# Two of the twelve adaptive-modulation parts moved from TensorE to VectorE, and their loads into the feed-forward stage

## The reference

```python
mod = jax.nn.silu(c) @ w_ada[l] + b_ada[l]                     # 1024 -> 6 * 1024
sh_m, sc_m, gt_m, sh_f, sc_f, gt_f = jnp.split(mod, N_MOD, axis=-1)
h = modulate(rms_norm(x, g_mix[l]), sh_m, sc_m)
y = token_mixer(h, ...)        # dilated attention and an mLSTM, joined, times w_out
x = x + gt_m[:, None, :] * y
h = modulate(rms_norm(x, g_ffn[l]), sh_f, sc_f)
x = x + gt_f[:, None, :] * swiglu(h, w_gate[l], w_up[l], w_down[l])   # inner width 2816
```

## Time and profile before

| | us |
|---|---|
| median of 3 runs (1412.06 to 1413.28) | 1412.82 |
| the profiled execution | 1411.05 |
| its span, first to last instruction | 1409.0 |
| TensorE busy in it | 1273.0 (90%) |
| VectorE busy | 726.7 (52%) |
| ScalarE busy | 238.8 (17%) |
| GpSimd busy | 324.6 (23%) |

### The profile page before, as it was taken

The page is one execution under the profiler, slowest core; times in us unless marked ns, Lnnn a source line. Parts: engine busy times, 40 slices in busy tenths (PEclk is TensorE's granted clock), DMA queues, the critical chain, the costliest instruction groups (busy, mean ns, idle before and its releaser), DMA issues.

```text
span 1409.0 us, 12608 instructions
## 1 busy us (share of the span) xinstructions
PE 1273.0 (90%) x4558; PEld 730.9 (52%) x4558; DVE 726.7 (52%) x1752; ACT 238.8 (17%) x611; POOL 324.6 (23%) x273
## 2 busy tenths in 40 slices
PE   7999999988988878788799887878999899999998
PEld 6757554574554444333333333333465468988743
DVE  3664623178777777787786865653255242100001
ACT  2132221121111111112221112112112421000000
POOL 0100000024544544354444454540000000000000
PEclk9999999999999999899999998999999989999999
DMA  8534576369999999999999999995344723552530
GB/s 289 176 123 180 179 277 245 120 269 421 390 419 421 421 416 420 416 421 401 417 422 421 411 415 421 420 422 216 120 166 166 263 78 120 179 180 95 204 145 34
DMA packets 98380, 398.72 MB, mean 283 GB/s; under 512 B 6353, under 2 KB 9809, under 8 KB 65425
## 3 DMA queue, kind: packets, MB, share of 16 engines
q0 software_dynamic: 37376, 270.29, 46.4%
q1 hardware_dynamic: 60944, 127.65, 25.4%
HBM read 396.86 MB, written 1.05 MB: 282 GB/s over the span
## 4 chain that ended last, share of the span: by engine, by line
PE 60%; DMA 22%; DVE 12%; issue 2%; ACT 2%; POOL 1%; DVEq 0%; SPq 0%; ACTq 0%
DMA big<-in_peer_uv,idx_t 21%; PE ps L497 16%; PE ps L509 14%; PE ps L747 11%; DVE big L1763 6%; PE ps L998 5%; PE ps L716 2%; PE ps L686 2%; PE ps L962 2%; PE ps L523 1%; PE ps L589 1%; POOL big L1364 1%; PE ps L486 1%; DMA wring<-in_w_ada 1%; ACT rows L1185 1%
## 5 line engine op out<-in xcount | busy, mean ns | idle before, releaser
L747 PE MATMUL ps<-big,rows 128*128 128x512 f32 x1024 | 489.0, 634 | 105.4 <-ACT rows L1185 105.4
L1364 POOL DMA_INDIRECT big<-in_peer_uv,idx_t x256 | 312.0, 1219 | 388.9 <-PE ps L747 323.5
L747 PEld LDWEIGHTS ps<-big,rows 128*128 128x128 f32 x1024 | 202.7, 203 | 374.0 <-issue 374.0
L1763 DVE CUSTOM_DVE_ANT_0 big<-big 128x1024 f32<-128x1024 f32 x256 | 307.8, 1225 | 145.5 <-DMA big<-in_peer_uv,idx_t 142.5
L497 PE MATMUL ps<-wring,big 128*128 128x512 f32 (+1 forms) x560 | 240.5, 586 | 2.6 <-DMA wring<-in_w_in 1.1
L509 PE MATMUL ps<-big,wring 128*128 128x256 f32 x896 | 195.7, 381 | 1.0 <-DVE big L1418 1.0
L509 PEld LDWEIGHTS ps<-big,wring 128*128 128x128 f32 x896 | 171.2, 191 | 25.3 <-issue 1.9
L497 PEld LDWEIGHTS ps<-wring,big 128*128 128x128 f32 x560 | 105.6, 191 | 125.8 <-issue 121.0
L1179 ACT ACTIVATE small<-small 128x4 f32<-128x4 f32 x64 | 13.2, 206 | 514.7 <-DVE small L1768 514.7
L1185 ACT ACTIVATE rows<-const,small 128x128 f32<-128x128 f32 x256 | 81.8, 390 | 19.2 <-DVE small L1772 18.0
L998 PE MATMUL ps<-wring,big 128*128 128x512 f32 x176 | 75.7, 592 | 0.0
(11 more groups left out here) (241 smaller groups left out, 921.9 us busy)
## 6 DMA issues: line engine op xcount, KB each, us to landing
wring<-in_w_in SPq DMA_DIRECT2D x17, 2048.0 KB, 8.3
wring<-in_w_ada SPq DMA_DIRECT2D x12, 2048.0 KB, 8.5
wring<-in_w_gate SPq DMA_DIRECT2D x5, 2048.0 KB, 7.7
wring<-in_w_up SPq DMA_DIRECT2D x5, 2048.0 KB, 7.7
wring<-in_w_down SPq DMA_DIRECT2D x5, 2048.0 KB, 7.6
wring<-in_w_out SPq DMA_DIRECT2D x4, 2048.0 KB, 15.1
wring<-in_peer_wq SPq DMA_DIRECT2D x4, 2048.0 KB, 8.0
big<-in_peer_uv,idx_t POOLq DMA_INDIRECT x256
```

What stands on the lines that cost most here:

```text
L747: last = nc.tensor.matmul(banks[h], diag[:, k % DIAGS, :], v_part[:, ring_at(k), h * 512:(h + 1) * 512], start=False, stop=(k % SLOTS == S ...
L1364: pool.indirect_dma_start(pair_ring[:, ring_at(k), :], None, a["peer_uv"], bass.IndirectOffsetOnAxis(idx_t[:, k:k + 1], 0))\
L1763: nc.vector.tensor_tensor_reduce(u_part[:, ring_at(k), :], u_part[:, ring_at(k), :], h_t[:, b, :], 1.0, 0.0, ALU.mult, ALU.add, a_dot[:, i ...
```

## The change

- The tiles ada10 and ada11 leave their place behind ada9 in the list of loads. ada10 now stands behind up1 and ada11 behind up2 (`FF_ADA = {1: 10, 2: 11}`), in the same ring.
- TensorE no longer computes them. DVE does, by `gate_part`: behind its work on gate1/up1 (and on gate2/up2) it waits for the tile and runs one tensor_scalar and seven scalar_tensor_tensor over 128 x 512 elements, each multiplying a 128-row slice of the tile with its column of silu(c) and adding to mod_part(i). Each of the eight waits for the one before.
- The sum over the 128 rows is still a matmul, with ones in all rows as the stationary operand (`one.to_broadcast([P, P])`), behind up2 for part 10 and behind up3 for part 11. ACT moves its result behind its tanh of gate2 and gate3.
- SP's wait for the slot of an ada tile is on the new semaphore ada_made, which DVE raises.
- POOL raises mod_ready after each of its two additions; DVE needs the first before gt_m is used and the second before the last additions.
- As the list of products is shorter by ada10 and ada11 in the mixer and has ada_row 10 and 11 later, all products behind m_S get other banks.

```diff
+FF_ADA = {1: 10, 2: 11}
...
-    t += [("in2_og", KD, 512, "w_in_2", 0, 512 * 6)] + ada[8:12]
+    t += [("in2_og", KD, 512, "w_in_2", 0, 512 * 6)] + ada[8:10]
...
         t += [(f"gate{i}", KD, w, "w_gate", 0, 512 * i), (f"up{i}", KD, w, "w_up", 0, 512 * i)]
+        if i in FF_ADA:
+            t += [ada[FF_ADA[i]]]
...
                     before = TILES[n - W_SLOTS][0]
-                    if before.startswith("down"):
+                    if before in ("ada10", "ada11"):
+                        sp.wait_ge(ada_made, int(before[3:]) - 9)
+                    elif before.startswith("down"):
...
             def ada_row(i):
 
-                wait_moved(pe, f"ada{i}")
+                if i >= 10:
+                    pe.wait_ge(ada_made, i - 9)
+                else:
+                    wait_moved(pe, f"ada{i}")
                 o = begin("ada_row", i)
-                nc.tensor.matmul(o, group_sum, mod_part(i), start=True, stop=True).then_inc(product_done, 1)
+                nc.tensor.matmul(o, one.to_broadcast([P, P]) if i >= 10 else group_sum, mod_part(i), start=True,
+                                 stop=True).then_inc(product_done, 1)
...
-            ada_part(10)
-            ada_part(11)
             ada_row(8)
             ada_row(9)
...
             attended(0)
-            ada_row(10)
-            ada_row(11)
             probs_turned(1)
...
                 by_cols(f"up{i}", TILES[TILE_NO[f"up{i}"]][2], hT2)
+                if i - 1 in FF_ADA:
+                    ada_row(FF_ADA[i - 1])
...
-            ada_moves(10)
-            ada_moves(11)
             move(mod_part(8), "ada_row", 8)
...
-                if b:
-                    move(mod_part(10), "ada_row", 10)
-                    move(mod_part(11), "ada_row", 11)
...
                     nc.scalar.activation(ff_e, bank((f"gate{i}", h)), ACT.Tanh, scale=0.5).then_inc(ff_exp, 1)
+                if i - 1 in FF_ADA:
+                    move(mod_part(FF_ADA[i - 1]), "ada_row", FF_ADA[i - 1])
...
-                if j == 0:
-                    link(last)
-            last.then_inc(mod_ready, 1)
+                last.then_inc(mod_ready, 1)
+                pool.wait_ge(mod_ready, j + 1)
...
+            def gate_part(i):
+
+                n = TILE_NO[f"ada{i}"]
+                slot = n % W_SLOTS * TILE
+                w = wring[:, slot:slot + TILE].rearrange("p (c n) -> p c n", c=KD)
+                to = mod_part(i)
+                dve.wait_ge(tile_landed[n % W_SLOTS], 16 * (n // W_SLOTS + 1))
+                link(ts(to, w[:, 0, :], c_s[:, 0:1], None, ALU.mult))
+                for c in range(1, KD - 1):
+                    link(stt(to, w[:, c, :], c_s[:, c:c + 1], to, ALU.mult, ALU.add))
+                stt(to, w[:, KD - 1, :], c_s[:, KD - 1:KD], to, ALU.mult, ALU.add).then_inc(ada_made, 1)
...
+                if i in FF_ADA:
+                    gate_part(FF_ADA[i])
+            dve.wait_ge(mod_ready, 2)
```

More of the change, by code:

```diff
@@ L175, in product_list @@
     p += [("m_cols",), ("m_M", 0), ("m_M", 1)] + [("m_S", h) for h in range(GH)]
-    p += [("ada10",), ("ada11",), ("ada_row", 8), ("ada_row", 9)]
-    p += [("d_PT", 0, 0, q) for q in range(2)] + [("d_Y", 0), ("ada_row", 10), ("ada_row", 11)]
+    p += [("ada_row", 8), ("ada_row", 9)]
+    p += [("d_PT", 0, 0, q) for q in range(2)] + [("d_Y", 0)]
     p += [("d_PT", 1, sb, q) for sb in range(NB) for q in range(2)]
@@ L186, in product_list @@
             p += cols(n, 2 if i < 5 else 1)
+        if i - 1 in FF_ADA:
+            p += [("ada_row", FF_ADA[i - 1])]
     p += [("down", b, h) for b in range(NB) for h in range(2)]
@@ L379, in two_blocks @@
         ple_exp, mod_ready, x_ready = sem("ple_exp"), sem("mod_ready"), sem("x_ready")
-        modc_ready = sem("modc_ready")
+        modc_ready, ada_made = sem("modc_ready"), sem("ada_made")
         d_norm, d_max, d_probs, cat_ready = sem("d_norm"), sem("d_max"), sem("d_probs"), sem("cat_ready")
```

## The result

| | before | after |
|---|---|---|
| median, us | 1413.10 (6 runs, 1412.06 to 1413.68) | 1403.65 (6 runs, 1401.05 to 1406.13) |
| the profiled execution, us | 1411.05 | 1404.53 |
| its span, us | 1409.0 | 1402.7 |
| ratio, 95% interval | | 0.9932 (0.9919 to 0.9945) |

The changed kernel is 9.5 us faster by the medians, 6.5 by the two profiled executions. The forecast was 1405.5 in 1402.2 to 1409.0.

The account below looks back on a forecast made before the run. TensorE, busy 1273 of 1409 us, was taken as the bound, with a chain of waits at the mixer's end. 1411.05 - 9.1 (mixer chain) + 1.8 (clock) + 1.8 (row sums) = 1405.5 us, range 1402.2 to 1409.0.

Parts of the forecast that it names:

- ada10 and ada11 out of the mixer: Mixer's end on TensorE: without these parts and their row sums there, m_num 0 starts 8.35 us earlier.
- the 0.2 counted against the gain: Mixer, d_Y 0: ACT's four moves take 2.1 us, so it starts at about 1116.4 and not 1116.2.
- POOL's hold: DVE's small tensor_scalar before the second division waits for POOL's bias addition; moving that gains 0.75 us, m_den 1 late next.
- Row sums: Feed-forward stage on TensorE, which has no gap: two row sums return at 0.9 us each, +1.8 us, perhaps not hidden.
- DVE's parts: Feed-forward stage on DVE: eight steps of 0.69 us, 5.8 us a part, covered by 112 us of idle time, cost 0.
- The loads: Feed-forward stage: tiles ada10 and ada11 delay no gate load, at least 6 us of slack, cost 0 to +0.5 us.
- third rival: Feed-forward stage stalls: long DVE steps delay gate4's load; part 11 needs 20 us; at 3.5 us a step, 1413.5; chance 0.03.
- The clock: Mixer's end: the lower clock level starts with d_Y 1, so catT waits 2.0 us for it; taken as +1.8 us.
- The clock held through the 3 us of standstill: Mixer before the change: the clock held through standstill and 9 us of narrow work behind it; evidence against an all-low narrow stretch.
- second rival: Lower clock over the whole narrow stretch, row sum 9 to d_Y 1: +11.9 us, 1415.6 or 1417.4; chance 0.05.
- The sum from the median: Whole kernel, from the median without the clock term: 1412.82 - 9.1 + 1.8 = 1405.5 us.

Follow-up runs that it names:

- e1: The kernel before with only POOL's second bias addition moved behind up2 and mod_ready raised after each addition; 1410.13 us, 0.9984 of the kernel before.
- e2: The changed kernel without the two row sums of parts 10 and 11 and their moves on ACT; 1402.75 us, 0.9934 of the kernel before.
- e3: The changed kernel without parts 10 and 11 at all: no loads, DVE work or row sums; 1401.61 us, 0.9917 of the kernel before.
- e6: The changed kernel with each of DVE's two parts made 23 steps long and not 8; 1405.28 us, 0.9959 of the kernel before.
- c1: The changed kernel again, unaltered, timed beside the kernel before on the same chip; 1402.63 us, 0.9927 of the kernel before.
- b2: The kernel before, unaltered, one more execution traced as a second sample; 1413.46 us.
- b3: The kernel before, unaltered, one more execution traced as a third sample; 1411.56 us.
- e5: The changed kernel with two unused 512-column matmuls added on TensorE between m_den 1 and d_Y 1; 1401.51 us, 0.9920 of the kernel before.
- e9: The kernel before with TensorE making parts 10 and 11 between m_den 1 and d_Y 1, row sums behind first catT, POOL's second addition late; 1400.89 us, 0.9925.
- e7: The changed kernel with parts 8 and 9 moved on TensorE between m_den 1 and d_Y 1, their row sums behind the first catT; 1400.41 us, 0.9914.
- e8: The changed kernel with part 8 on DVE ahead of m_M, part 9 on TensorE behind m_den 1, row sums behind first catT; 1397.27 us, 0.9894.

## Why the prediction was right, point by point

- **ada10 and ada11 out of the mixer, -8.35.** m_num 0 came 8.6 us earlier in the profiled pair (24.4 to 15.8). ACT did release d_Y 0, but its four moves took 2.02 us and not 2.1 and d_Y 0 followed at once, so the 0.2 counted against the gain did not come.
- **POOL's hold, -0.75 more, m_den 1 next.** Right, with e1 as the test: 0.17 us, released by m_den 1. The second division started at 21.1 and not 30.5 from in2_og's end, 9.35 earlier against 9.1. The Trainium skill, SBUF — State Buffer, section "Who interferes with whom", says that a tensor_scalar can take the pair of ports that DVE shares with GpSimd, and that the one who comes second is blocked for the whole instruction of the other; the trace and e1 agree, with 1.53 and 0.17 us.
- **Row sums, +1.8, bare.** 1.72; e2 and e3 show that it is all the stage pays.
- **DVE's parts, 0.** Right. A part is 6.0 us and not 5.8: the scalar_tensor_tensor takes 0.75 and not 0.69, the tensor_scalar 0.48 and not 0.69.
- **The loads, 0, "at least 6 us of slack" and the third rival's 20 us for part 11.** The cost was right. The third rival looked at the wrong load: e6 shows that gate3 behind ada11 is the tight one, since its load queues behind ada11's wait and is in flight together with it (12.9 us to land). The slack that ends first is about 8 us on part 10; the 20 on part 11 were not reached by e6. The step that POOL held, which that rival names as the one slow step "of that size", is 128 x 4 and not 128 x 512.
- **The clock, +1.8: this term was mis-sized.** In the profiled pair it was 0. d_Y 1 at the lower level held catT back by 0.4 us, not 2.0, as the level fell only some 1.5 us into it (granted clock 0.63 over 5.59 us); catT with its moves (2.44 against 2.70) and out2 (15.71 against 15.88) gave that back. With the term gate1 would start at 100.15 - 9.1 + 1.8 = 92.85; five of the six traces of this mixer have it at 89.5 to 91.3, and c1 at 94.0. Without the term the sum is 1403.7, and the median measured is 1403.65. That closeness is luck: the sum starts from one execution of before, which was faster than all six timed beside the changed kernel, and the profiled execution after it took 1404.53.
- **"The clock held through the 3 us of standstill."** True of the one execution that was read, not of the two others. That was evidence used against the second rival, and it was thin. It also hid a gain: with the standstill gone, the 2.0 us that b2 and b3 lose behind it are gone too. The sum from the median, 1412.82 - 9.1 + 1.8, missed that.
- **The second rival (the lower level over the whole narrow stretch)** did not come in any trace. c1, e3 and e5 had 3.4 us of the lower level early, but in m_S, where it cost 1.7 us, and none from there to m_den 1. The rival's bound was mis-added as well: 8.8 us before the end of d_Y 1 at 1129.1 is 1120.3, the end of d_PT 1, and not 1118.3. The Trainium skill, TensorE: Matmul & The Clock Gate, Part 4: PE-mode transpose, says that a transpose doesn't count as busy for the clock in the same way; no run here separates that.

## What to carry to other kernels

Work that nothing nearby needs should not stand ahead of a chain that runs over several engines, even if each piece is small: look for the point at which one engine waits for another and put the wide work there (e9, e7, and e8, which adds a part on DVE), before moving it to another engine. Where a queue's wait is handed to a new engine, the load to check is the one behind the waiting one, and with both transfers in flight. One trace doesn't tell where the clock falls: take two or three of the kernel before, and price the lower level as a range.

## What the runs showed of the hardware

- The clock fell in m_S, early in it, in five of the fourteen traces (c1, e1, e3, e5, e8). c1, the stretch from the ada products to m_M and then m_S:

```profile
1104.85:1110.58 5.73, 5.73 (x45) 2.58 (x45) 0.82 (x2) 2.07 (x5) 0.00 (x0) 1.00 0.82 277
1110.58:1115.06 4.48, 4.48 (x18) 3.95 (x18) 2.96 (x9) 2.87 (x8) 0.00 (x0) 0.62 1.05 392
```

  TensorE had been busy without a break ahead of it, with m_cols and m_M, whose stationary operands have four rows. m_S took 4.48 us and not 2.8. A busy engine is no guarantee of the upper level.
- With 1.8 to 3.6 us of wide products between m_den 1 and d_Y 1 the level stayed up through d_Y 1 and out2 in four traces of four (e5, e7, e8, e9; out2 13.7 to 14.0 us). Without them it fell in d_Y 1, catT or out2 in all ten (out2 15.4 to 16.8 us).
- With two loads of 2 MB issued 0.4 us apart, the second took 12.9 us to land; the median of gate loads before was 7.7 (e6).
- A DVE step of 128 x 4 elements took 1.53 us under POOL's addition and 0.17 without it (e1).
